# Low-rank products and the keys' chain behind the last level, attention's keys and values copied out by ScalarE, decay picks moved

## What is computed

```python
pl = hl @ w_in[layer]; pc = hc @ w_in[layer]              # latent and context rows, 256 each
al, bl, cl = split(pl, [A_PROJ, A_PROJ + B_PROJ])         # three mixers: HGRN2, RWKV7, attention
a_lat = hgrn2_mixer(...)                                  # decays by levels, then a group norm
b_lat = rwkv7_mixer(...)                                  # w, a and g through low-rank products, keys kk normalised per head
c_lat = neighbourhood_attention(...)                      # queries nq, keys nk, values nv
xl = xl + g1l * (concat([a_lat, b_lat, c_lat]) @ w_out)
```

## Time and profile before

| | us |
|---|---|
| median of 3 runs (2169.6 to 2178.95) | 2176.22 |
| the profiled execution, whole | 2175.41 |
| its span (first to last instruction) | 2173.6 |
| PE busy | 1883.1 (87%) |
| DVE busy | 1604.6 (74%) |
| ACT busy | 1115.4 (51%) |
| POOL busy | 143.9 (7%) |

### The profile page before, as it was taken

The page is one execution under the profiler, slowest core; times in us unless marked ns, Lnnn a source line. Parts: engine busy times, 40 slices in busy tenths (PEclk is TensorE's granted clock), DMA queues, the critical chain, the costliest instruction groups (busy, mean ns, idle before and its releaser), DMA issues. The chain is left out here.

```text
span 2173.6 us, 32136 instructions
## 1 busy us (share of the span) xinstructions
PE 1883.1 (87%) x12662; PEld 1588.1 (73%) x12662; DVE 1604.6 (74%) x2097; ACT 1115.4 (51%) x1326; POOL 143.9 (7%) x150
## 2 busy tenths in 40 slices
PE   2888879998688878998699974998899999999998
PEld 2766668986676667996587754886788788787786
DVE  6787757976597765995548669656688688787886
ACT  2644436651564435663264342223577677676774
POOL 0000000000000000000006406500000000000000
PEclk9989899998998898999799986998899999999998
DMA  7577626655576744566421200003599799798897
GB/s 271 200 253 242 225 87 243 242 199 179 185 239 234 245 143 184 211 226 231 159 96 66 88 0 12 22 20 135 185 348 373 278 360 376 274 374 319 313 375 257
DMA packets 158134, 460.32 MB, mean 212 GB/s; under 512 B 10928, under 2 KB 13616, under 8 KB 155440
## 3 DMA queue, kind: packets, MB, share of 16 engines
q1 hardware_dynamic: 158000, 458.51, 58.9%
HBM read 457.42 MB, written 1.05 MB: 211 GB/s over the span
## 5 line engine op out<-in xcount | busy, mean ns | idle before, releaser
L212 DVE TENSOR_TENSOR me_wlow<-me_w,me_whigh 128x2048 fp32r<-128x2048 f32 (+1 forms) x203 | 452.0, 2247 | 107.5 <-ACT me_whigh L207 107.2
L207 ACT ACTIVATE me_whigh<-me_w 128x2048 fp32r<-128x2048 f32 (+1 forms) x203 | 380.3, 1885 | 137.8 <-PE ps L220 131.2
L218 PE MATMUL ps<-me_whigh,me_xhigh 128*128 128x512 f32 x512 | 207.5, 405 | 11.8 <-PEq L119 11.8
L218 PE MATMUL ps<-up_xhigh,ffn_whigh 128*128 128x256 f32 x704 | 202.4, 287 | 8.6 <-DVE ffn_wlow L212 7.0
L220 PE MATMUL ps<-me_whigh,me_xlow 128*128 128x512 f32 x528 | 208.7, 395 | 0.0
L219 PE MATMUL ps<-me_wlow,me_xhigh 128*128 128x512 f32 x512 | 202.5, 395 | 0.0
L219 PE MATMUL ps<-up_xlow,ffn_whigh 128*128 128x256 f32 x704 | 201.6, 286 | 0.0
L220 PE MATMUL ps<-up_xhigh,ffn_wlow 128*128 128x256 f32 x704 | 201.4, 286 | 0.0
L212 DVE TENSOR_TENSOR ffn_wlow<-ffn_w,ffn_whigh 128x2048 fp32r<-128x2048 f32 (+1 forms) x72 | 149.3, 2110 | 29.0 <-ACT ffn_whigh L207 28.7
L212 DVE TENSOR_TENSOR mix_wlow<-mix_w,mix_whigh 128x1024 fp32r<-128x1024 f32 (+2 forms) x116 | 140.1, 1211 | 29.8 <-ACT mix_whigh L207 29.8
L207 ACT ACTIVATE ffn_whigh<-ffn_w 128x2048 fp32r<-128x2048 f32 (+1 forms) x72 | 123.1, 1758 | 69.1 <-PE ps L220 69.1
(11 more groups left out here) (658 smaller groups left out, 4204.7 us busy)
## 6 DMA issues: line engine op xcount, KB each, us to landing
me_w<-w_exp_gate SPq DMA_DIRECT2D x34, 2048.0 KB, 9.6
me_w<-w_exp_up SPq DMA_DIRECT2D x34, 2048.0 KB, 10.2
me_w<-w_exp_down SPq DMA_DIRECT2D x32, 2048.0 KB, 10.3
mix_w<-w_mix SPq DMA_DIRECT2D x108, 512.0 KB, 3.8
mix_ada_w<-ada_w SPq DMA_DIRECT2D x96, 512.0 KB, 4.9
ffn_w<-ffn_w_up SPq DMA_DIRECT2D x20, 2048.0 KB, 7.8
ffn_ada_w<-ffn_ada_w SPq DMA_DIRECT2D x48, 512.0 KB, 5.5
ffn_w<-ffn_w_down SPq DMA_DIRECT2D x8, 2048.0 KB, 7.8
```

Source lines behind the costliest of these rows:

```text
L207: return nc.scalar.activation(high, x, ACT.Copy)
L212: return nc.vector.tensor_tensor(low, x, high.bitcast(F32), ALU.subtract)
L218: nc.tensor.matmul(out, lh, rh, start=start, stop=False)
```

## The change

The eight low-rank products stand around and between the two weighings, with the gate products behind them and the sums of squares behind nk3. The parts of the norm, kk, scans and logs are planned right behind; clamp, reciprocal and kk times kn follow, and the splits of nv come between them. All tiles of nk and nv are copied out by ACT. The picks are made in `setup_dve` of the first stage, in a tile of their own, and the wait of product `b` goes.

```diff
+            yield 13.2
+            for hp in range(2):
+                nc.vector.tensor_scalar(keys["pick"][:, hp], consts["head_pick"], fv["r_k"][:, hp:hp + 1], None, ALU.mult)\
+                    .then_inc(picked, 1)
...
                 for t in tiles[name]:
-                    if t % 2 == parity:
+                    if (t % 2 if name == "nq" else 1) == parity:
...
-                yield t_low + 1.2 * i
+                yield t_low[i]
...
-                yield t_low + 9.6 + 1.2 * t
+                yield t_weigh + 0.8 + 0.05 * t
...
-                yield t_low + 12.0 + 1.2 * hp
+                yield t_weigh + 5.7 + 0.05 * hp
...
-                yield t_low + 1.2 * i + 1.0
+                yield t_low[i] + 0.05
...
-                yield t_keys + 18.0 + 1.5 * d
+                yield t_weigh + 7.5 + 2.0 * d
...
-                yield t_keys + 1.5 * hp
+                yield t_weigh + 1.3 + 0.1 * hp
...
-                    yield max(t_low + 3.4 + 1.2 * (2 * d + hp), t_keys + 3.0 + 1.3 * (2 * d + hp))
+                    yield t_weigh + 3.6 + 0.4 * d + 0.2 * hp
...
-                yield t_keys + 8.5 + 3.7 * d
+                yield t_weigh + 4.6 + 1.0 * d
...
-            yield t_keys + 16.0
+            yield t_weigh + 10.5
...
-            yield t_keys + 24.0
+            yield t_weigh + 11.0
...
-                yield t_keys + 25.5 + 4.0 * d
+                yield t_weigh + 16.0 + 6.0 * d
...
-                yield t_keys + 28.2 + 4.0 * d
+                yield t_weigh + 16.5 + 6.0 * d
...
-                yield t_weigh + 1.0 * t
+                yield t_weigh + 0.2 + 0.2 * t
...
-        t_weigh = when(len(SPANS), 9.5)
-        t_low, t_keys = t_weigh + 1.5, t_weigh + 10.5
+        t_weigh = when(len(SPANS), 7.3)
+        t_low = [t_weigh + at for at in (0.05, 0.1, 0.3, 0.35, 0.5, 0.55, 0.6, 0.65)]
...
-                yield t_weigh + 1.6 + 0.5 * t
+                yield t_weigh + 0.45 + 0.25 * t
...
-            yield t_weigh + 6.0
+            yield t_weigh + 2.0
...
-            yield t_weigh + 3.4
+            yield t_weigh + 1.0
...
-            yield t_weigh + 8.0
+            yield t_weigh + 3.0
...
-                pe.wait_ge(picked, 2)
...
-            for hp in range(2):
-                V.tensor_scalar(pick[:, hp], consts["head_pick"], fv["r_k"][:, hp:hp + 1], None, ALU.mult).then_inc(picked, 1)
```

More of the change, by code:

```diff
@@ L2227, in ended @@
                 eng.wait_ge(done, pieces.count(name, t if name not in tiles else 3))
-        ctx_here, started, mu_made = sem("ctx_here"), sem("started"), sem("mu_made")
+        ctx_here, started, mu_made, picked = sem("ctx_here"), sem("started"), sem("mu_made"), sem("picked")
         final_here, vectors_here, rest_here = sem("final_here"), sem("vectors_here"), sem("rest_here")
@@ L2388, in low_act @@
             for t in range(TT):
-                yield t_low + 10.6 + 1.2 * t
+                yield t_weigh + 1.5 + 0.05 * t
                 act.wait_ge(low, 9 + t)
@@ L2392, in low_act @@
             for hp in range(2):
-                yield t_low + 13.0 + 1.2 * hp
+                yield t_weigh + 6.0 + 0.05 * hp
                 act.wait_ge(kk_summed, hp + 1)
@@ L2667, in levels_act @@
                     nc.scalar.activation(ks[:, d], exc[:, d, :, keys], ACT.Exp, scale=2.0).then_inc(exped[d], 1)
-            yield when(len(SPANS), 8.0)
+            yield when(len(SPANS), 7.0)
             act.wait_ge(multiplied[1], 2 * len(SPANS))
@@ L2711, in levels_dve @@
                 for d in range(2):
-                    yield when(n, (5.2, 7.8)[d])
+                    yield when(n, (5.2, 7.8 if b < 2 * P else 7.0)[d])
                     if b < P:
@@ L2730, in levels_dve @@
             flat_rs = rs.rearrange("p t h -> p (t h)")
-            yield t_weigh + 3.4
+            yield t_weigh + 1.0
             dve.wait_ge(squared, TT)
             nc.vector.tensor_reduce(flat_rs, sq.rearrange("p t h d -> p (t h) d"), AX_X, ALU.add).then_inc(out_own, 1)
-            yield t_weigh + 4.6
+            yield t_weigh + 1.2
             dve.wait_ge(out_own, 1)
             nc.vector.tensor_scalar(flat_rs, flat_rs, 1.0 / HD, EPS, ALU.mult, ALU.add).then_inc(meaned, 1)
-            yield t_weigh + 8.0
+            yield t_weigh + 3.0
             dve.wait_ge(root, 1)
             nc.vector.reciprocal(flat_rs, flat_rs).then_inc(out_own, 1)
-            yield t_weigh + 8.5
+            yield t_weigh + 3.2
             dve.wait_ge(out_own, 2)
@@ L2744, in levels_dve @@
                                         rs[:, t, :].unsqueeze(2).to_broadcast([P, A_HEADS, HD]), ALU.mult).then_inc(out_own, 1)
-            yield t_weigh + 9.7
+            yield t_weigh + 3.4
             dve.wait_ge(out_own, 4)
@@ L2845, in second_recurrences @@
     small = Carver(core.sb(mem, "rw_small", [P, 180])[:, :])
-    bon, st, pick = small(TT, B_HEADS), small(2, TT, B_HEADS), small(2, 2)
+    bon, st, pick = small(TT, B_HEADS), small(2, TT, B_HEADS), keys["pick"]
     top, total, rs = small(TT * C_HEADS), small(TT * C_HEADS), small(TT + NT4, C_HEADS)
@@ L3184, in second_recurrences @@
                        (an[:, 1], a2t[:, 1])]
-        grown, fed, picked, ahead_made, reduced = (sem(n) for n in ("grown", "fed", "picked", "an_made", "na_reduced"))
+        grown, fed, ahead_made, reduced = (sem(n) for n in ("grown", "fed", "an_made", "na_reduced"))
         def core_pe(pe):
@@ L4345, in second_block @@
                         kt=carve(2, 2, NTOK), rt=carve(2, 2, NTOK), k2=carve(2, 2, NTOK), up=carve(3 * A_W),
+                        pick=core.sb(inner, "rw_pick", [P, 2, 2])[:, :, :],
                         tot=core.sb(inner, "rw_total", [P, 2, 2, 8])[:, :, :, :], gt=core.sb(inner, "rw_gate", [P, TT, A_W])[:, :, :])
```

## The result

The changed kernel takes 2166.16 us, median of 20 runs (2158.57 to 2172.09, but for one), against 2177.2 us for the kernel before (20 runs, 2166.93 to 2181.07). The ratio is 0.995, 95% interval 0.9937 to 0.9964: 11 us (8 to 14) faster, where 10.7 saved and 2165.0 were forecast. The profiled execution after took 2166.36 us, span 2164.6.

What follows compares the result with a forecast made beforehand. The first stage was taken to end in the keys' chain on VectorE and GpSimd, not in products. The next stage at 1302.9 instead of 1313.65 saves 10.7, picks and ScalarE's copies 0: 2165.0 us, range 2160.5 to 2171.5.

Steps and rivals of the forecast that it cites:

- Step 1: First stage up to the norm's reciprocal: reordered low-rank products, weighings and sigmoids bring it to 1261.8 from 1265.44.
- R: Time of the norm's reciprocal in the first stage, forecast at 1261.8 where it was 1265.44.
- Step 2: VectorE's queue from R without a pause: closing group 1 ends at R + 36.9, GpSimd's last operations at R + 39.6.
- The turns: VectorE and GpSimd do not overlap on such operations, so GpSimd's two of 2.33 add 4.7 to VectorE's queue.
- Step 3: nv products on PE: waits for nk's banks, 5.9, cost nothing; last copy R + 40.0, 10.7 saved.
- rival B: PE's clock falls in the stop before nv3, which takes 9.4 not 5.6; gain 6.9, time 2168.7; chance 0.18.
- Step 4: nk and nv copies: VectorE loses four of 0.6, already counted in its order; ScalarE gains four of 0.6.
- Step 5: Picks moved out of the second stage's head: gain taken as 0, bounds 0 and 3.6.
- Rival C: Moving the picks does pay at the second stage's head, 2.3 to 3.6 more: 2161.4 to 2162.7; chance 0.12.
- D: Slower: clock stays at 1.2 GHz through nv1 to nv3, products become the end, 2177.8 to 2178.6; chance 0.03.
- E: Part of the order fails, such as ScalarE's long queue delaying R by 3 to 5 us: 2168 to 2170; chance 0.15.

Runs made afterwards that it cites:

- kt_dve: Changed kernel with GpSimd's two products kt times kk given to VectorE behind kk times kn; 2157.81 us, ratio 0.9917 to the kernel before, stretch 65.69 us.
- nk_first: Changed kernel with ScalarE's exponentials planned behind all four nk copies; 2161.12 us, ratio 0.9917 to the kernel before, stretch 66.39 us.
- after_again: Changed kernel run again unaltered, for a second profile; 2166.34 us, ratio 0.9952 to the kernel before, stretch 68.03 us.
- no_copies: Changed kernel with the even tiles of nk and nv copied by VectorE again; 2162.73 us, ratio 0.9938 to the kernel before, stretch 67.62 us.
- picks_only: Kernel before with only the two picks moved to the first stage's setup; 2174.89 us, ratio 0.9998 to the kernel before.
- no_picks: Changed kernel with the picks back at the head of the second stage; 2161.94 us, ratio 0.994 to the kernel before.
- no_picks_an: Changed kernel with picks back in the second stage and GpSimd's pair an = a2 times k2 on VectorE; 2168.68 us, one run, no ratio.
- best1: Changed kernel with exponentials behind nk copies, nv1 and nv2 splits before the reciprocal, kt on VectorE, sa on ScalarE; 2160.23 us, ratio 0.9917 to the kernel before.
- best1_again: The same program as best1, run again beside the changed kernel; 2161.31 us, ratio 0.9928 to the kernel before, stretch 61.80 us.

## Why the prediction was right, step by step

**Step 1, R.** Forecast 26.3 behind `far` (1261.8 less 1235.51), measured 26.00. The table load is followed by the root at its end (1266.82 + 1.28, root at 1268.12), so the sum by the rows held and the 1.4 us that the Trainium skill (ScalarE: Activation LUTs, What ACT_TABLE_LOAD costs) would have added with its drain did not appear: the root follows the load's end by 0.02.

**Step 2, VectorE's queue.** Forecast to end at R + 36.9, measured 1304.68 less 1268.36 = 36.3; GpSimd R + 39.6, measured 39.05. The turns are in the rows: sw took 3.42 and the two `sa` 2.90, where 1.22 and 0.88 are usual; that is 4.2 of the 4.7 that I had added. kt_dve shows the same from the other side.

**Step 3, products.** Forecast R + 40.0 for the last copy, measured 39.5. Next stage forecast at R + 41.1, measured 40.5: **10.7 forecast, 11.6 measured**; of the difference R gave 0.3 and the queue and what stands behind it 0.6. The stops for nk's banks came as named, 3.32 and 1.29 against 3.7 and 2.2, and nk_first shows that they cost 0.1: "nothing" was right.

What failed in this step is the stop of 3.5 before nv3. It was 1.10 in one profile and 2.90 in the other. The clock that fell in nv0's stops held nv0's tiles at half speed, so nv1 began at R + 20.9 and R + 19.1 where the sum has R + 18.4, and that ate into the stop. I had this only as an argument against rival B. 0.6 of it is a slip of the sum: R + 7.5, the stops of 5.9 and four tiles of 1.4 make R + 19.0. The slip does not touch the path, since nv3 waited for VectorE all the same. **Rival B** is real, but smaller than I priced it: 1.5 us, not 3.8, and in one profile of four. That it was not the forecast's own case is luck in part: nothing in my sum said how long the half clock would hold nv0. I had taken 8.3 us of half speed from the earlier trace rows; in after_again the clock was back 3.3 us after work resumed. The Trainium skill (TensorE: Matmul & The Clock Gate, HAM oscillation) has, in a kernel that waits for transfers, every burst behind such a wait start cold. The second profile agrees before nv3, with 0.80 for the first matmul behind 2.90; nv0's first matmul behind 2.41, 0.50 in both profiles, and nv3's in the first, 0.50 behind 1.10, do not.

**Step 4, copies.** Valued inside the order at 4 x 0.6 less on VectorE; measured 1.1 (no_copies). Only the two nk copies lie in the middle of the queue; I had not said which of the four were on the path. The old order with ScalarE's copies gives 0.1, or 0.5 at an equal clock.

**Step 5, picks.** Forecast 0, bounds 0 and 3.6; measured 0.3 in every profile of each kind (6.97 to 6.67), nothing in the time. Rival C falls by picks_only and no_picks; no_picks_an shows whose time it was.

**Rivals D and E** did not happen: in the changed kernel's two profiles the clock came back before nv1, in no profile of the new order did more than about one piece of 24 matmuls run at half speed, and R was 0.3 early. Of the chances, the 0.46 for faster is more than its stated parts, 0.12 and half of 0.52, which make 0.38; nothing in the working gives the rest.

**What was not taken apart.** The order was tried as a whole. The rows put 11.24 of its gain down to the earlier R and the missing pause of 7.31, but no run moves one group of planned times alone.

**What is not the change.** Outside the stretch the two profiles differ by more than the change is worth in places: `far` is copied 6.85 later after, and from the third stage's first load to the end it took 666.99 against 672.23. Over all profiles of this study the former ranges from 1229 to 1244, the latter from 664 to 672, the second stage itself from 186 to 193. Why these parts vary so was not tried. The last part may not be free of the change: it is 670.2 to 672.5 in the three profiles of the old order and 663.8 to 670.1 in the eleven others. The measured 11.0 of the medians fits 11.6 of the stretch plus 0.3 of kh's pair, less what the half clock takes in some executions; but the median alone could not tell it within 3 us.

## What to carry to other kernels

Where a stage ends in a long chain on one engine while another waits for nothing, write out that engine's queue from the first operation that can start earlier to the last, with the operations of any engine that takes turns with it; its sum gave this gain within 1 us, and each product or copy beside it mattered only as load on that queue. Before moving a small operation that shows a long time, look at what runs beside it: the time may belong to the neighbour and pass to whatever comes next. Judge a change of some microseconds in a kernel of milliseconds by a stretch between two fixed rows in which no data is loaded, and take it more than once: three profiles of the same stretch agreed within 0.03 us (66.50 to 66.53) and a fourth was 1.5 longer, by the clock alone.

## What the runs showed of the hardware that was not expected

- VectorE and GpSimd alternated one instruction each on operations of 128x1024 in fp32: kh's two of 1.22 took 5.65 and GpSimd's two of 2.33 took 5.65 at the same time, and two operations on two elements a partition took 4.66 beside the pair and 0.56 without it. I had expected the turns, not that they would be this regular: the kh pair took 6.66 to 6.68 in all eight profiles in which GpSimd's pair met kh.
- The same program had the granted clock at 0.50 for nv3's first 3.3 us in one execution and not in another. After a stop of 2.90 it fell, after 1.10 it did not.
- Behind nearly the same stop before nv0 the clock did three things: in best1 (2.42) it was at 0.50 for 3.3 us, in best1_again (2.41), the same program, it stayed at 1.00, and in no_picks (2.41) it fell within the second matmul and was back only 13 us later.
